# A three-layer hybrid model on one core: the third mixing's first four tiles from operands without the root, and rotary tables and lambda inside the feed-forward block

## What is computed

```python
x = x + 0.5 * swiglu(rms_norm(x, ffn1_norm), w_gate, w_up, w_down)      # f1g, f1u, f1d
h = rms_norm(x, mix_norm)            # x * rsqrt(mean(x*x) + 1e-6) * gain
z = h @ w_in                         # 48 tiles of 128 columns: in3
g_a, g_b, z_uv, z_q, z_k, z_v = split(z)
u, v = split(gelu(z_uv))             # tiles 16 to 19 and 20 to 23
v = layer_norm(v); y_a = u * (causal w_s @ v + b_s)
cos, sin = cos(positions * inv), sin(positions * inv)
q, k = rope(rms_norm(z_q), cos, sin), rope(rms_norm(z_k), cos, sin)
lam = exp(sum(lq1 * lk1)) - exp(sum(lq2 * lk2)) + 0.2
y_b = norm((softmax(q1 k1) - lam * softmax(q2 k2)) v)       # 8 heads
m = sigmoid(g_a) * (y_a @ a_proj) + sigmoid(g_b) * (y_b @ b_proj)
x = x + m @ w_out; x = x + 0.5 * swiglu(rms_norm(x, ffn2_norm), ...)
```

## Time and profile before

| | |
|---|---|
| Median of 3 runs | 3093.42 us (3091.96 to 3094.5) |
| Span of the profiled execution | 3089.4 us |
| PE busy | 2977.7 us, 96% of the span |
| PE weight loads | 2385.2 us, 77% |
| DVE, ACT, POOL busy | 1605.5, 1078.7, 1412.1 us |
| Mean granted clock of TensorE | 0.988 of full speed |
| DMA read from memory | 243.18 MB, 79 GB/s |

### The profile page before, as it was taken

The page is one execution under the profiler, slowest core; times in us unless marked ns, Lnnn a source line. Parts: engine busy times, 40 slices in busy tenths (PEclk is TensorE's granted clock), DMA queues, the critical chain, the costliest instruction groups (busy, mean ns, idle before and its releaser), DMA issues.

```text
span 3089.4 us, 42486 instructions
## 1 busy us (share of the span) xinstructions
PE 2977.7 (96%) x16912; PEld 2385.2 (77%) x16912; DVE 1605.5 (52%) x3295; ACT 1078.7 (35%) x1781; POOL 1412.1 (46%) x1817
## 2 busy tenths in 40 slices
PE   6998999999999999999999999999899999999999
PEld 5777777787888887767877778888776768788887
DVE  5766567566566416559744453330466773433310
ACT  4443333333322223323324433222354553332221
POOL 3553344344556544314334364555543334655554
PEclk9999999999999999999999999999999999999999
DMA  3211112112344432102112222333321112232232
GB/s 123 83 55 60 57 55 69 55 56 82 117 149 144 129 96 66 36 21 69 36 48 75 69 82 96 96 94 101 101 69 61 58 59 81 84 96 96 97 103 88
DMA packets 72358, 248.02 MB, mean 80 GB/s; under 512 B 8160, under 2 KB 8544, under 8 KB 72032
## 3 DMA queue, kind: packets, MB, share of 16 engines
q1 hardware_dynamic: 72160, 245.30, 24.8%
HBM read 243.18 MB, written 2.10 MB: 79 GB/s over the span
## 4 chain that ended last, share of the span: by engine, by line
PE 84%; DVE 12%; ACT 2%; issue 1%; POOL 1%; DMA 0%; SPq 0%; DVEq 0%; ACTq 0%; POOLq 0%
PE bank L1054 23%; PE bank L1056 22%; PE bank L1055 22%; PE bank L1088 3%; PE bank L1102 3%; PE bank L1533 1%; PE bank L1065 1%; PE bank L1551 1%; DVE sm L1617 1%; DVE sm L1619 1%; PE bank L1542 1%; PE bank L1372 1%; DVE sm L1621 1%; POOL t L2943 1%; DVE t L1764 1%
## 5 line engine op out<-in xcount | busy, mean ns | idle before, releaser
L2910 POOL TENSOR_TENSOR R<-W,R 128x256 fp32r<-128x256 f32 x1715 | 1287.9, 784 | 1540.5 <-ACT R L2518 1540.5
L1054 PE MATMUL bank<-u,R 128*128 128x512 f32 (+1 forms) x3440 | 1393.9, 405 | 27.2 <-DVE u L1720 8.3
L1056 PE MATMUL bank<-u,R 128*128 128x512 f32 (+1 forms) x3440 | 1348.8, 392 | 0.0
L1055 PE MATMUL bank<-u,R 128*128 128x512 f32 (+1 forms) x3440 | 1347.8, 392 | 0.0
L1054 PEld LDWEIGHTS bank<-u,R 128*128 128x128 f32 (+1 forms) x3440 | 649.2, 189 | 182.5 <-issue 15.9
L1056 PEld LDWEIGHTS bank<-u,R 128*128 128x128 f32 (+1 forms) x3440 | 648.6, 189 | 142.4 <-issue 0.4
L1055 PEld LDWEIGHTS bank<-u,R 128*128 128x128 f32 (+1 forms) x3440 | 650.3, 189 | 127.5 <-issue 4.8
L2518 ACT ACTIVATE R<-W 128x1024 fp32r<-128x1024 f32 (+2 forms) x454 | 452.3, 1002 | 143.3 <-PE bank L1056 136.8
L2548 ACT ACTIVATE u<-t 128x512 fp32r<-128x512 f32 x126 | 78.3, 630 | 322.9 <-DVE t L1742 249.1
L1753 DVE SCALAR_TENSOR_TENSOR X<-bank,X 128x512 f32<-128x512 f32 x32 | 22.1, 692 | 260.2 <-PE bank L1056 260.2
L1720 DVE TENSOR_TENSOR u<-t,u 128x512 fp32r<-128x512 f32 x126 | 97.3, 782 | 100.5 <-ACT u L2548 99.8
(11 more groups left out here) (389 smaller groups left out, 2748.4 us busy)
## 6 DMA issues: line engine op xcount, KB each, us to landing
W<-in_in SPq DMA_DIRECT2D x48, 512.0 KB, 3.3
W<-in_ff_in SPq DMA_DIRECT2D x44, 512.0 KB, 3.3
W<-in_g_qkv SPq DMA_DIRECT2D x24, 512.0 KB, 3.3
...
```

Source lines behind the costliest of these rows:

```text
L1054: e.matmul(b[0:cols, :], wh, hi, start=(k == 0), stop=False)
L1055: e.matmul(b[0:cols, :], wh, lo, start=False, stop=False)
L1056: i = e.matmul(b[0:cols, :], wl, hi, start=False, stop=(k == KT - 1))
L2910: i = e.tensor_tensor(R[q % NH][:, 1024 + a:1024 + b], W[p % NW][:, a:b], R[q % NH][:, a:b].bitcast(F32), SUB)
```

## The change

1. Tiles 20 to 23 are multiplied from X times gain without the root: `xg` with number 7 (same gain as norm 5) runs beside f1d, into tiles 0 to 15. `nsum` and `rms` come after half of tile 20, `rmsp` after half of tile 21. `rb` copies the root into tile 41. `gv` becomes two steps: DVE multiplies bank by root, ACT applies Gelu in place. The banks of this part are 0 to 3, and each transpose comes later.
2. `h` of norm 5 still makes the operands with the root, now for the other 44 tiles of in3, into tiles 16 to 31. It reads the root from tile 41 and not from bank 7, all low halves are on DVE and none on POOL, and its steps stand between the tiles 20 to 22.
3. `rope`, `lam` and `rotg` and their DMAs (`load diff`) run beside f1d; the two Sin activations (`sine`) stand behind its last tile. `load gmlp` stays at the root.
4. The last transpose `gvt` 3 moves behind tile 40, into the planned part. Tiles of SBUF are renumbered. The planner gets the same steps with `gvt` 3 added, and its order of the mixing comes out otherwise.

```diff
-SQ = (69, 70, 71)
+SQ, SQ5 = (69, 70, 71), (57, 58, 59)
+HB = {5: 16}
+ROOT = {5: 41}
...
-ROPE_C, ROPE_S = 16, 17
-M3 = tuple(range(18, 26))
-GG3 = tuple(range(26, 34))
+ROPE_C, ROPE_S = 32, 33
+ANGLE = (64, 65)
+M3 = tuple(range(2, 10))
+GG3 = tuple(range(10, 16)) + (0, 1)
-F_PI, F_AN, F_N, F_LAM = 34, 35, 36, 37
+F_PI, F_AN, F_N, F_LAM = 60, 61, 62, 63
-    "yg": (tuple(G_T[f % 2] for f in range(4)), (26, 27, 28, 29), (30, 31, 32, 33)),
-    "ydiff": (YD[0:6], H0[0:6], H1[0:6]),
-    "ydiff2": (YD[6:8], H0[6:8], H1[6:8]),
+    "yg": (tuple(G_T[f % 2] for f in range(4)), GG3[0:4], GG3[4:8]),
+    "ydiff": (YD[0:6], tuple(range(16, 28, 2)), tuple(range(17, 28, 2))),
+    "ydiff2": (YD[6:8], (28, 30), (29, 31)),
...
 AFTER = {
+    "gvt": lambda j: [("dense", "in3", 40, 1)],
...
-        out += [("xg", n, j)] if n in (1, 4, 6) else []
+        out += [("xg", n, j)] if n in (1, 4, 6) else [("xg", 7, j)] if n == 5 else []
+        if n == 5:
+            out += {0: [("load", "diff")], 1: [("rope", 0)], 2: [("rope", 1)], 3: [("lam",)], 7: [("rotg",), ("sine", 0), ("sine", 1)]}.get(j, [])
...
-    O += norm(5, [("load", "gmlp"), ("load", "diff")])
-    for j in range(4):
-        O += tiles("in3", 20 + j, ("gv", j)) + [("gvt", j - 1)] * (j > 0)
-    O += [("gvt", 3), ("gw",), ("rope", 0), ("rope", 1), ("lam",), ("rotg",)]
-    mlp = [("gn", m) for m in range(4)] + [("gnn",)] + [("gn2", m) for m in range(4)]
+    one, two, four = tiles("in3", 20), tiles("in3", 21), tiles("in3", 23)
+    O += [("pool", (0, 1, 2, 3))] + one[:2] + [("nsum", 5, 7), ("rms", 5)] + one[2:] + two[:2] + [("rmsp", 5), ("rb", 5), ("load", "gmlp")]
+    O += [("gv", 0), ("h", 5, 0), ("h", 5, 1)] + two[2:] + [("gv", 1)] + [("h", 5, k) for k in range(2, 5)]
+    O += tiles("in3", 22) + [("gvt", 0), ("gv", 2)] + [("h", 5, k) for k in range(5, 9)]
+    O += four[:2] + [("gvt", 1)] + four[2:] + [("gvt", 2), ("gv", 3), ("gw",), ("pool", (0, 1))]
+    mlp = [("gvt", 3)] + [("gn", m) for m in range(4)] + [("gnn",)] + [("gn2", m) for m in range(4)]
...
-                s = BR.act if j < 16 else GM.act if j < 24 else AT.act
+                s = BR.act if j < 16 else GM.act if j < 20 else GM.dve if j < 24 else AT.act
...
-            def operand(name, k):
+            def operand(name, j, k):
                 if name in NORM_OF:
-                    n = NORM_OF[name]
-                    w.wait_ge(*(NM.pool if k % 2 and n in (0, 5) else NM.dve).at("lo", n, k))
-                    return r(2 * k), r(2 * k + 1)
+                    n = 7 if name == "in3" and 20 <= j < 24 else NORM_OF[name]
+                    w.wait_ge(*(NM.pool if k % 2 and n == 0 else NM.dve).at("lo", n, k))
+                    a = HB.get(n, 0) + 2 * k
+                    return r(a), r(a + 1)
...
-                    w.wait_ge(*NM.pe.at("r", n))
+                    w.wait_ge(*(NM.act.at("rb", n) if n == 5 else NM.pe.at("r", n)))
...
                         w.wait_ge(*NM.act.at("hi", n, k - 3))
-                        w.wait_ge(*(NM.dve if k % 2 or n == 3 else NM.pool).at("lo", n, k - 3))
-                    e.scalar_tensor_tensor(out=t(SQ[k % 3]), in0=X[:, k, :], scalar=gain(n, k), in1=bank[NB[n]], op0=MUL,
+                        w.wait_ge(*(NM.dve if k % 2 or n in (3, 5) else NM.pool).at("lo", n, k - 3))
+                    e.scalar_tensor_tensor(out=t((SQ5 if n == 5 else SQ)[k % 3]), in0=X[:, k, :], scalar=gain(n, k), in1=t(ROOT[5]) if n == 5 else bank[NB[n]], op0=MUL,
                                            op1=MUL).then_inc(*NM.dve.up("h", n, k))
-                if k and (k % 2 or n == 3):
+                if k and (k % 2 or n in (3, 5)):
...
                     else:
-                        e.tensor_tensor(r(2 * k - 1), t(SQ[(k - 1) % 3]), r(2 * k - 2).bitcast(F32),
+                        e.tensor_tensor(r(HB.get(n, 0) + 2 * k - 1), t((SQ5 if n == 5 else SQ)[(k - 1) % 3]), r(HB.get(n, 0) + 2 * k - 2).bitcast(F32),
                                         SUB).then_inc(*NM.dve.up("lo", n, k - 1))
...
+            def gv(j):
+                w.wait_ge(*PN.pe.at("dense", "in3", 20 + j))
+                w.wait_ge(*NM.act.at("rb", 5))
+                if j >= 3:
+                    w.wait_ge(*GM.pe.at("vt", j - 3))
+                e.tensor_tensor(t(G_T[j % 3]), bank[BANK["in3", 20 + j]], t(ROOT[5]), MUL).then_inc(*GM.dve.up("got", "in3", 20 + j))
...
-                an, nn, o = t(F_AN), t(F_N), t((ROPE_C, ROPE_S)[n])
+                an, nn, o = t(F_AN), t(F_N), t(ANGLE[n])
...
-                        e.activation(r(2 * k), t(SQ[k % 3]), ACT.Copy).then_inc(*NM.act.up("hi", n, k))
+                        e.activation(r(HB.get(n, 0) + 2 * k), t((SQ5 if n == 5 else SQ)[k % 3]), ACT.Copy).then_inc(*NM.act.up("hi", n, k))
...
             def rb(n):
                 w.wait_ge(*NM.pe.at("r", n))
-                e.activation(t(RB), bank[NB[n]], ACT.Copy).then_inc(*NM.act.up("rb", n))
+                e.activation(t(ROOT.get(n, RB)), bank[NB[n]], ACT.Copy).then_inc(*NM.act.up("rb", n))
...
             def gv(j):
-                w.wait_ge(*PN.pe.at("dense", "in3", 20 + j))
-                if j >= 3:
-                    w.wait_ge(*GM.pe.at("vt", j - 3))
-                e.activation(t(G_T[j % 3]), bank[BANK["in3", 20 + j]], ACT.Gelu).then_inc(*GM.act.up("got", "in3", 20 + j))
+                w.wait_ge(*GM.dve.at("got", "in3", 20 + j))
+                e.activation(t(G_T[j % 3]), t(G_T[j % 3]), ACT.Gelu).then_inc(*GM.act.up("got", "in3", 20 + j))
...
-            def rope(n):
-                o = t((ROPE_C, ROPE_S)[n])
+            def sine(n):
                 w.wait_ge(*DF.dve.at("rope", n))
-                e.activation(o, o, ACT.Sin).then_inc(*DF.act.up("rope", n))
+                w.wait_ge(*PN.pe.at("dense", "f1d", 7))
+                e.activation(t((ROPE_C, ROPE_S)[n]), t(ANGLE[n]), ACT.Sin).then_inc(*DF.act.up("rope", n))
...
-                if n != 3 and k and k % 2 == 0:
+                if n not in (3, 5) and k and k % 2 == 0:
...
                 if what == "gmlp":
                     w.wait_ge(*NM.pe.at("r", 5))
+                    w.wait_ge(*DF.dve.at("lam"))
+                    w.wait_ge(*DF.act.at("rope", 1))
...
                 if what == "diff":
-                    w.wait_ge(*NM.pe.at("r", 5))
+                    w.wait_ge(*PR.dve.at("lo", "hid1", NFF - 1))
...
```

More of the change, by code:

```diff
@@ L954, in x_ready @@
                 return s_x[k // 2], 16
-            return RS.dve.at("got", {1: "w_out", 2: "ff_dn", 3: "ff_dn", 4: "w_o", 5: "f1d", 6: "out3"}[n], k)
+            return RS.dve.at("got", {1: "w_out", 2: "ff_dn", 3: "ff_dn", 4: "w_o", 5: "f1d", 6: "out3", 7: "f1d"}[n], k)
         def x_before(name, j):
@@ L962, in gain @@
                 return small["gc"][:, k:k + 1]
-            return P({0: "norm_mix_w", 1: "norm_ffn_w", 4: "ffn1_norm", 5: "mix_norm", 6: "ffn2_norm"}[n], k)
+            return P({0: "norm_mix_w", 1: "norm_ffn_w", 4: "ffn1_norm", 5: "mix_norm", 6: "ffn2_norm", 7: "mix_norm"}[n], k)
         def ready(tag, k):
@@ L1050, in dense @@
                     at = (j % GROUP.get(name, 1) * KT + k % 8) * cols
-                    hi, lo = operand(name, k)
+                    hi, lo = operand(name, j, k)
                     w.wait_ge(*PN.pool.at("lo", key))
@@ L1694, in h @@
                         w.wait_ge(*NM.act.at("hi", n, k - 3))
-                        w.wait_ge(*(NM.dve if k % 2 or n == 3 else NM.pool).at("lo", n, k - 3))
-                    e.scalar_tensor_tensor(out=t(SQ[k % 3]), in0=X[:, k, :], scalar=gain(n, k), in1=bank[NB[n]], op0=MUL,
+                        w.wait_ge(*(NM.dve if k % 2 or n in (3, 5) else NM.pool).at("lo", n, k - 3))
+                    e.scalar_tensor_tensor(out=t((SQ5 if n == 5 else SQ)[k % 3]), in0=X[:, k, :], scalar=gain(n, k), in1=t(ROOT[5]) if n == 5 else bank[NB[n]], op0=MUL,
                                            op1=MUL).then_inc(*NM.dve.up("h", n, k))
-                if k and (k % 2 or n == 3):
+                if k and (k % 2 or n in (3, 5)):
                     w.wait_ge(*NM.act.at("hi", n, k - 1))
                     if n == 3:
-                        e.scalar_tensor_tensor(out=r(2 * k - 1), in0=t(SQ[(k - 1) % 3]), scalar=small["mod"][:, k - 1:k],
-                                               in1=r(2 * k - 2).bitcast(F32), op0=ADD, op1=SUB).then_inc(*NM.dve.up("lo", n, k - 1))
+                        e.scalar_tensor_tensor(out=r(HB.get(n, 0) + 2 * k - 1), in0=t((SQ5 if n == 5 else SQ)[(k - 1) % 3]), scalar=small["mod"][:, k - 1:k],
+                                               in1=r(HB.get(n, 0) + 2 * k - 2).bitcast(F32), op0=ADD, op1=SUB).then_inc(*NM.dve.up("lo", n, k - 1))
                     else:
-                        e.tensor_tensor(r(2 * k - 1), t(SQ[(k - 1) % 3]), r(2 * k - 2).bitcast(F32),
+                        e.tensor_tensor(r(HB.get(n, 0) + 2 * k - 1), t((SQ5 if n == 5 else SQ)[(k - 1) % 3]), r(HB.get(n, 0) + 2 * k - 2).bitcast(F32),
```

(8 more changed lines are left out.)

4 lines of the change are left out of this document (2 added, 2 removed).

## The result

The changed kernel takes 3075.86 us (median of 4 executions, 3074.26 to 3078.82), the kernel before beside it 3092.73 (3091.96 to 3094.5): a ratio of 0.9946, with an interval of 0.9933 to 0.9958. That is 16.9 us less. The forecast was 13.7 less, 3079.7, with a range of 3074 to 3087: right in sign and inside the range, 3 to 4 us short. The profiled execution has a span of 3073.4 us against 3089.4.

The account below looks back on a forecast made before the run. PE was taken as the bound, with time won only where it stands or runs at the lower clock. Gains of 11.5 + 1.7 + 0.5 = 13.7 us from 3093.4 gave 3079.7, range 3074 to 3087.

Parts of the forecast that it names:

- the last rival: In the mixing, PE stands, then runs 10 us at half speed, twice, losing over 19.9 us: 3100; chance 0.04.
- The front: From f1d's last matmul to tile 40: 26.7 us in place of 38.65, so 12.0 won.
- The deciding step: Before tile 40: DVE's multiply of tile 23, last of 20 instructions, frees its bank; tile 40 waits for it.
- The port's term: In the front's 16 `h` and low-half instructions: two SBUF inputs beside POOL add 1.6 us, between 0 and 6.7.
- the 7.8 us of the rival: In DVE's run: 16 instructions each wait 0.98 us half the time; gain 7.5, 3085.9; 0.04 of that rival's chance.
- 1.7 for v: Behind tile 40: PE's 2.17 us wait for ACT's copy of head 0's v shrinks to some 0.45, 1.7 won.
- 0.5 for the wait at 2277: In the mixing: PE's 1.13 us wait for DVE's backlog; half taken as won, 0.5 us, bounds 0 and 1.1.
- 0.5 for the last transpose: Behind tile 40: tile 23's transpose now comes there, taking 0.5 us off the front's 12.0.
- DVE as the bound in the sense of 6.7 us: In the front: port waiting of 6.7 us in place of 1.6, gain 8.6, 3084.8; chance 0.12.
- The order giving some back: In the mixing: new waits of 5 to 7 us where heads 0 and 1 end, 3085 to 3087; chance 0.16.
- The root's wait stays: At tiles 20 to 23: ACT or weights late, PE stands, half the gain goes, about 3086; chance 0.06.
- Slower, with the clock falling twice: In the mixing: heads 2 and 3 start late, PE stands and drops to half speed twice, 3100; chance 0.04.

Follow-up runs that it names:

- the kernel with the operands alone: New front and new order, but tables and lambda left between tile 23 and the mixing as in the kernel before: 3090.35 us against 3093.35, ratio 0.9991.
- the run with the root in its bank: The changed kernel, but `h` reads the root from PSUM bank 7 as before: 3075.83 us against 3093.83 for the kernel before, 0.9944.
- the repeat: The changed kernel measured again, nothing altered: 3078.84 us against 3093.83 for the kernel before, ratio 0.9953.
- the kernel with the tables alone: The kernel before with only `rope`, `lam`, `rotg` and the two Sin moved beside f1d: 3088.75 us against 3093.35, ratio 0.9985.

## Why the prediction was right, and where its sum was off

**What bounds the kernel.** Right: PE's idle time at the entrance was what the change could win. The lower clock, which the prediction counted as the second place where time can be won, was worth 0.9 us there, all in the root's spread. The 2.3 us that the last rival takes from the first matmuls of tile 20 at the lower clock are not there: from its first matmul to its last piece the tile took 7.84 us with it and 7.83 without.

**The front.** 12.0 us were forecast, 12.0 measured. The intervals and costs taken from the earlier trace rows and, for a transpose, from the earlier trace rows gave the place of each row within 0.2 us: the sum 2.97 behind f1d's last matmul, the root's spread at 9.37 (forecast 9.3), the start of DVE's run at 11.1 (forecast 11.0). The deciding step, DVE's multiply of tile 23 as the bound of tile 40, ended at 26.6 (forecast 26.6). Three parts of it were less sure than they looked:

- The root was taken to be ready 4.06 us after the sum's start, as in the earlier trace rows, with 2.2 us to spare. It was ready after 5.8, with 0.6 to spare. The cause is that four of the Newton steps of 4 columns, from 2210.11 on, ran beside POOL's splits and took 0.59 to 0.68 us in place of 0.17; two between them took 0.15. In the two kernels without the tables in f1d, ACT has no Sin there, POOL starts sooner, and the root is 0.92 us late. The forecast named the Sin as a thing in ACT's queue, and did not see that it also holds POOL back and so helps the root.
- The port's term, 1.6 us, came out near: eight `h` at 0.864 and eight low halves at 0.821, against 0.70, are 2.3. The reason given was only half right: POOL was busy for 4.35 us of the run's 15.5 and not for half of it, and the four instructions beside it took 0.5 more each.
- That the run of 20 came out to a tenth is partly luck. The forecast was 14.0 (20 at 0.70) and 1.6 for the port, 15.6 in all; the run took 15.5. But neighbours start 0.60 to 0.66 us apart and not 0.70, so the 20 alone are some 12.7; 0.5 is waiting for ACT, which the sum had at nothing, and some 2.1 is the port, by starts (four at 1.15 in place of 0.64). Errors of 1.3, 0.5 and 0.5 us cancelled.

**The rule on the port.** The forecast held the Trainium skill (SBUF — State Buffer, "Who interferes with whom") to be too severe, since 0.42 us was less than one POOL instruction of 0.74. The rows now speak for the rule. POOL's instruction takes 0.70 us here (5.60 by 8 in the kernel with the operands alone), and from 2210.47 to 2213.94 DVE begins six steps of 4 columns, 0.69 us apart, so one per instruction of POOL; the wait is what is left of the running one, not all of it. The same page of the Trainium skill lists `tensor_scalar` among the operations that can take the shared port; the trace fits that, 0.66 to 0.72 us for one of 4 columns. And it says that an instruction with at most one SBUF input, outside its two-port modes, does not contend, which the run with the root in its bank shows: 0.73 us beside POOL. What kept the 7.8 us of the rival from coming was that POOL worked beside four of the 16 instructions and not eight, and that each of the four lost 0.5 us and not 0.98.

**Behind the front.** Forecast 1.7 for v, 0.5 for the wait at 2277, less 0.5 for the last transpose, net 1.7; tile 40 to the end measured 1.7 less. By terms: the wait for v fell by 1.92 (2.17 to 0.25). The wait of 1.13 for L2300 has its like at 2280.53, with 1.36 us. In the old order, with the tables moved, all waits for that line are 0.5 less (3.8 to 3.3); in the new order they are 1.1 less (3.8 to 2.7), but other waits are longer, so the term of 0.5 can't be read by itself. The new order was worth nothing, as taken. The total of this stretch says little: it is 842.6 in the first profile and 839.8 to 840.7 in the repeat and in three other kernels with the new front and order, but 844.3 and 846.9 in the two profiles of the old front with the old tables. So 1.7 is the least difference among them and 7.1 the most; the 1.9 at head 0's v is what a wait shows.

**The tables cost nothing beside f1d.** Right, as the kernel with the tables alone shows: no wait in f1d, and a front of 38.6. But the step that gave them their worth failed: it credited moving them with 2.2 us (1.7 for v, 0.5 at 2277) and the new front with 11.5 by itself. The runs show that the two can't be added. Alone the tables win 4.6 us and the operands 3.0, together 15 to 17. In place of 2.2 us, leaving the tables where they were costs 9.8 us behind tile 40 once the front is short. The forecast for the whole was right because both were made at once; the forecast for a half, the operands alone at 9 to 12, failed by 6 to 9.

**The total.** 12.0 in the front and 1.7 behind it make 13.7 of the 16.0 by which the two profiled spans differ; the other 2.3 lie ahead of f1d's last matmul (2204.14 against 2206.42), where the change only adds `xg` and the tables beside f1d, and PE has no wait in f1d in either profile. The repeat's profile has that point at 2210.11. So these 2.3 can't be put down to the change. What lies around the span was taken as 4.0 us, from a median and one span; each execution's time less its own span is 1.8 (3075.25 - 3073.4); both kernels had it alike, so it does not touch the gain. Over both measurements the change is worth 15.0 to 16.9 us; beyond the 12.0 of the front and the 1.9 at head 0's v, 1 to 3 us have no place that was shown.

**The rivals.** DVE as the bound in the sense of 6.7 us: no. The order giving some back: no, it is neutral. The root's wait stays: no, though within 0.6 us. Slower, with the clock falling twice: no; but the kernel with the operands alone shows its mechanism, one wait of 9.82 us with a half-speed stretch behind it.
